# Cached latent pages loaded by SyncE, rotary products as 64x64 tiles, and paired key heads in a hybrid MLA/DSA step

## The reference, cut to what matters

```
k_nope = c_kv @ w_uk                 # 8 heads of 64, prompt: kn, kl
s = einsum('bqhc,bkc->bhqk', q_lat, c_kv) + einsum('bqhr,bkr->bhqk', q_pe, k_pe)
s = where(k_pos <= q_pos, s * MLA_SCALE, NEG_INF)     # k: 4096 cached, 8 new
p = softmax(s);  o_lat = einsum('bhqk,bkc->bqhc', p, c_kv);  o = o_lat @ w_uv
# cached c_kv (256) and k_pe (32) rows lie in pages of 128 tokens, 32 pages a batch,
# page numbers in page_table[8, 32]; branch B gathers 256 picked k and v rows a query
```

## Time and profile before

| what | value |
|---|---|
| median of three runs | 1749.62 us |
| profiled execution, its own time | 1741.32 us |
| its span | 1739.5 us |
| PE busy | 1626.2 us (93%) |
| DVE busy | 866.3 us (50%) |
| ACT busy | 421.6 us (24%) |
| POOL busy | 337.0 us (19%) |
| gate tiles on PE | 400.27 to 528.2 us |
| latent stage on PE | 531.36 to 806 us |
| DMA | 218.38 MB, mean 126 GB/s |

### The profile page before, as it was taken

How to read it: one execution, slowest core, us unless ns; L and a number is a source line. 1 busy time by engine, 2 the same in 40 slices (tenths; PEclk the granted TensorE clock), 3 DMA queues, 4 the chain that set the end, 5 groups by cost and what they waited for, 6 DMA issues and landing times.

```text
span 1739.5 us, 21664 instructions
## 1 busy us (share of the span) xinstructions
PE 1626.2 (93%) x8572; PEld 999.0 (57%) x8572; DVE 866.3 (50%) x1636; ACT 421.6 (24%) x1111; POOL 337.0 (19%) x348
## 2 busy tenths in 40 slices
PE   6999989999999898998687899999999999989998
PEld 3554444446776666665454566547777777744443
DVE  3448798998522887874877742222322323210011
ACT  2131312001015545644355531001111111100010
POOL 2000000010004777770555630000000000000000
PEclk9899989999999999998798899999999999999999
DMA  8311212142306788877555845302122122111100
GB/s 247 141 62 61 106 42 98 63 167 86 135 36 242 264 283 298 278 264 219 144 147 150 280 134 182 115 20 89 49 73 73 49 73 73 49 61 49 65 23 32
DMA packets 89846, 218.38 MB, mean 126 GB/s; under 512 B 13576, under 2 KB 37520, under 8 KB 83696
## 3 DMA queue, kind: packets, MB, share of 16 engines
q0 software_dynamic: 29168, 116.66, 20.2%
q1 hardware_dynamic: 59506, 93.24, 16.2%
q10 hardware_dynamic: 1072, 7.09, 1.4%
HBM read 199.99 MB, written 16.84 MB: 125 GB/s over the span
## 4 chain that ended last, share of the span: by engine, by line
PE 77%; DVE 9%; POOL 6%; issue 3%; DMA 3%; ACT 2%; ACTq 0%; SPq 0%; DVEq 0%
PE PS L630 13%; PE PS L2063 13%; PE PS L2108 11%; PE PS L2091 7%; PE PS L681 7%; POOL mem L1820 5%; PE PS L2040 4%; PE PS L1538 2%; PE PS L746 2%; PE PS L2017 2%; DVE mem L1732 2%; PE PS L1408 2%; DVE mem L1731 1%; PE PS L1051 1%; PE PS L2471 1%
## 5 line engine op out<-in xcount | busy, mean ns | idle before, releaser
L630 PE MATMUL PS<-mem 128*128 128x512 f32 (+3 forms) x580 | 234.8, 561 | 0.0
L2063 PE MATMUL PS<-mem 128*128 128x376 f32 x704 | 231.7, 481 | 0.0
L2108 PE MATMUL PS<-mem 128*128 128x512 f32 (+1 forms) x440 | 192.2, 599 | 1.4 <-DVE mem L2287 1.4
L2063 PEld LDWEIGHTS PS<-mem 128*128 128x128 f32 x704 | 131.0, 189 | 79.3
L630 PEld LDWEIGHTS PS<-mem 128*128 128x128 f32 (+1 forms) x580 | 100.5, 186 | 119.8 <-issue 119.5
L1820 POOL DMA_INDIRECT mem<-in_cache_dsa_k,mem x128 | 143.9, 1124 | 43.6 <-issue 38.4
L1820 POOL DMA_INDIRECT mem<-in_cache_dsa_v,mem x128 | 122.5, 957 | 145.4 <-PE PS L1520 113.1
L2108 PEld LDWEIGHTS PS<-mem 128*128 128x128 f32 (+1 forms) x440 | 80.7, 184 | 112.3 <-issue 110.7
L2091 PE MATMUL PS<-mem 128*128 128x216 f32 x704 | 135.8, 345 | 0.0
L2091 PEld LDWEIGHTS PS<-mem 128*128 128x128 f32 x704 | 129.2, 189 | 10.7
L2268 DVE TENSOR_SCALAR mem<-mem 128x528 f32<-128x528 f32 x22 | 12.2, 555 | 238.8 <-ACT mem L2171 238.8
(11 more groups left out here) (312 smaller groups left out, 2087.7 us busy)
## 6 DMA issues: line engine op xcount, KB each, us to landing
mem<-in_w_in SPq DMA_DIRECT2D x10, 2048.0 KB, 8.2
mem<-in_w_ffn_g SPq DMA_DIRECT2D x11, 1024.0 KB, 5.4
mem<-in_w_ffn_u SPq DMA_DIRECT2D x11, 1024.0 KB, 5.4
mem<-in_w_ffn_d SPq DMA_DIRECT2D x10, 1024.0 KB, 5.0
tmp_gates<-mem SPq DMA_DIRECT2D x16, 296.0 KB, 2.1
mem<-tmp_gates SPq DMA_DIRECT2D x16, 296.0 KB, 4.0
mem<-in_w_o SPq DMA_DIRECT2D x2, 2048.0 KB, 11.8
mem<-in_x_prompt SPq DMA_DIRECT2D x6, 512.0 KB, 13.6
```

Of the source, the lines that this page charges most:

```text
L630: ins = pe.matmul(PS[0:n, b[bank], out_at:out_at + width], left[:, k, cols], w[:, k, at:at + width], start=k == 0, stop=k == k_range - 1)
L2063: pe.matmul(PS[:, 3 * (f % 2) + j, 0:UP_A], w[:, k, :], h2T[:, k, 0:UP_A], start=k == 0, stop=k == KD - 1)
L2108: return pe.matmul(PS[0:TW[m], (5 * n + m) % 8, :], upT[:, f, token_cols(m)], w[:, i, :], start=f == 0, stop=f == NF - 1)
```

## The change: what it does

The page loads move from POOL to SP (`sp_kpe_load`, `sp_latent_load`): per group of 8 pages SP loads the page numbers into registers, checks their range, and issues one DMA of 16 partitions per page. Batch 0's groups stand behind gate stores 8 to 12, those of the batches 1 to 7 behind SP's sample loads. POOL keeps the k and v gathers alone. The rotary products of an odd chunk and the even one before it go through four 64x64 tiles in two phases, around the odd chunk's second half of dots. The new tokens' products of all batches are made once, in batch 0. `outputs(b-1)` come behind the second chunk, ACT's and DVE's orders follow. `kn` and `kl` take two heads at once. The wait for the gate stores is left to SP alone. Two ring slots and two reloads at the end of the stage (kT, vb) change places, and four turns of x come one unit later.

The diff, cut to its core:

```diff
-        units += [("wt", 0)] + [("kn", h) for h in range(H)] + [("kl", 0), ("ql", 0), ("ql", 1)]
+        units += [("wt", 0)] + [("kn", p) for p in range(H // 2)] + [("kl", 0), ("ql", 0), ("ql", 1)]
...
-                    ins = pe.matmul(PS[0:64, b[0], :], wuk[:, c, 64 * m:64 * m + 64], ckvT[:, c, 0:512],
+                    ins = pe.matmul(PS[:, b[0], :], wuk[:, c, 128 * m:128 * m + 128], ckvT[:, c, 0:512],
...
-        AHEAD = 3
+        AHEAD = 2
         ROWS_B = 0
-        K_FROM = 4
+        K_FROM = 1
...
-            for i in range(2):
-                eng.wait_ge(sem(f"gates_stored{i}"), upto(f"gates_stored{i}", len(gate_tiles) - 2 + i))
...
+        def sp_pages(sp, b, first, n):
+            return nc.values_load_multi_w_load_instructions(
+                I["page_table"][b:b + 1, first:first + n], engines=[mybir.EngineType.SP], min_val=0,
+                max_val=I["cache_mla_ckv"].shape[1] - 1)[1]
+        def sp_kpe_load(sp, b):
+            if b:
+                sp.wait_ge(sem("sturned"), upto("sturned", ("p", b - 1, 1)))
+            for k in range(4):
+                for i, page_no in enumerate(sp_pages(sp, b, 8 * k, 8)):
+                    src = I["cache_mla_kpe"][0, bass.ds(page_no, 1)].rearrange("o (p r) d -> (o p) (r d)", p=16)
+                    sp.dma_start(kpe_raw[16 * i:16 * i + 16, 256 * k:256 * k + 256], src).then_inc(
+                        sem("kpe_in"), tick("kpe_in", *((b,) if k == 3 and i == 7 else ()), by=16))
+        def sp_latent_load(sp, n):
+            b, k = n // 4, n % 4
             if n >= 8:
-                gp.wait_ge(sem("latents_used"), upto("latents_used", n - 8))
-            gp.indirect_dma_start(raw_slot(n), None, ckv_rows,
-                                  bass.IndirectOffsetOnAxis(ap=idx_ckv[:, b, j:j + 1], axis=0)).then_inc(
-                sem(f"ckv_in{n % 8}"), tick(f"ckv_in{n % 8}", n, by=16))
+                sp.wait_ge(sem("latents_used"), upto("latents_used", n - 8))
+            for i, page_no in enumerate(sp_pages(sp, b, 8 * k, 8)):
+                src = I["cache_mla_ckv"][0, bass.ds(page_no, 1)].rearrange("o (p r) c -> (o p) (r c)", p=16)
+                sp.dma_start(raw_slot(n)[16 * i:16 * i + 16, :], src).then_inc(
+                    sem(f"ckv_in{n % 8}"), tick(f"ckv_in{n % 8}", *((n,) if i == 7 else ()), by=16))
...
+                if i == 8:
+                    sp.wait_ge(sem("heads_stored"), upto("heads_stored"))
+                    sp_kpe_load(sp, 0)
+                if 9 <= i < 13:
+                    sp_latent_load(sp, i - 9)
...
+            wait_stored(sp, "vb")
+            for b in range(1, NB):
+                sp_kpe_load(sp, b)
+                for k in range(4):
+                    sp_latent_load(sp, 4 * b + k)
...
-            phase_a_done(pe)
+            pe.wait_ge(sem("turned_act"), upto("turned_act", "kb", 4, 0))
...
+                            ins = pe.matmul(PS[64 * u:64 * u + 64, k % 2, :], q2[f], latT(("c", b, k, u, f)), start=f == 0,
+                                            stop=False, skip_group_check=True)
+                        if k % 2 and f == 0:
+                            if k == 1:
+                                pe.wait_ge(sem("sturn_out"), upto("sturn_out", ("p", b, 1)))
+                                pe.wait_ge(sem("qpe_spread"), upto("qpe_spread", b))
+                            rotary(b, k, 0).then_inc(sem("rotary_half"), tick("rotary_half", b, k))
...
+                    if k % 2:
+                        pe.wait_ge(sem("rotary_half"), upto("rotary_half", b, k))
+                        rotary(b, k, 1).then_inc(sem("latent_dots"), tick("latent_dots", b, k))
+                        same(("latent_dots", b, k - 1), ("latent_dots", b, k))
+                    if k == 0 and b == 0:
+                        new_tokens()
...
+            def rotary(b, k, phase):
+                for q in range(2):
+                    for u in range(2):
+                        for half, r in enumerate((LO, HI)):
+                            c, i = k - 1 + (half + phase) % 2, 2 * half + q
+                            ins = pe.matmul(PS[64 * u:64 * u + 64, c % 2, 128 * i:128 * i + 128], qpe_z[r, b % 2, i, :],
+                                            kpeT[b % 2][r, 2 * c + u, :], start=False, stop=phase == 1,
+                                            skip_group_check=True)
+                return ins
...
+            def new_tokens():
+                for b in range(NB):
+                    new, q = slice(NT * b, NT * b + NT), slice(64 * b, 64 * b + 64)
+                    out = PS[0:64, 3, 64 + NT * b:64 + NT * b + NT]
+                    for f in range(2):
+                        pe.matmul(out, ql_s[:, f, q], ckv_new[:, f, new], start=f == 0, stop=False)
+                    ins = pe.matmul(out, qpe_s[0:32, q], kpe_new[0:32, new], start=False, stop=True)
+                ins.then_inc(sem("own_dots"), tick("own_dots"))
...
-        gather_times = [(5 * ((n - 8) // 4 + 1) + 3 + n % 4 / 2 if n >= 8 else 0, n, None) for n in range(3, 4 * NB)]
-        gather_times += [(max(1, K_FROM + (q - 4) * (5 * NB - K_FROM) / NS), q, q) for q in range(NS)]
-        gather_order = [x[1:] for x in sorted(gather_times, key=lambda x: (x[0], x[1]))]
...
-            for n, q in gather_order:
-                if q is None:
-                    gp_latent_load(gp, n)
-                else:
-                    gp_gather(gp, "k", q)
+            for q in range(NS):
+                gp_gather(gp, "k", q)
```

More of the change, by code:

```diff
@@ L160, in trunk @@
         idx_row = K.take(NB, dtype=U32)
-        idx_ckv = K.take(NB, 4, dtype=U32)
+        K.take(NB * 4)
         small = K.take(64)
@@ L249, in trunk @@
         vb_at = qb_at + 2 * 4 * NCOL
-        slots = [C2.take(2048) for _ in range(4)]
-        slots[3:3] = [mem[:, vb_at:vb_at + 2048]]
+        slots = [C2.take(2048) for _ in range(4)] + [mem[:, vb_at:vb_at + 2048]]
         slots += [C.take(2048) for _ in range(3)]
@@ L267, in trunk @@
         R = Region(mem, picks_at, picks_at + ROW)
+        own = mem[0:64, picks_at:picks_at + NB * NT].rearrange("p (b n) -> p b n", b=NB)
         low, up, keep, page_f, off_f = (R.take(TOPK_S) for _ in range(5))
@@ L724, in wait_stored, with gates_done @@
                 eng.wait_ge(sem(f"stored_{name}_p"), upto(f"stored_{name}_p", 4))
+        def gates_done(eng):
+            for i in range(2):
+                eng.wait_ge(sem(f"gates_stored{i}"), upto(f"gates_stored{i}", len(gate_tiles) - 2 + i))
         def phase_a_done(eng):
@@ L991, in dots @@
                         close(b - 2)
+                    if b == 0 and k == 0:
+                        wait_unit_read(pe, ("gt", len(gate_tiles) - 1))
                     if k >= 2:
@@ L1019, in dots @@
                         pe_sturn(pe, ("n", b), [phys[0:64, 128 * f:128 * f + 128] for f in range(2)], 64)
-                pe.wait_ge(sem("scored"), upto("scored", b, 2))
-                new = slice(NT * b, NT * b + NT)
-                for f in range(2):
-                    pe.matmul(PS[0:64, 0, 0:NT], q2[f], ckv_new[:, f, new], start=f == 0, stop=False)
-                pe.matmul(PS[0:64, 0, 0:NT], qpe_s[0:32, 64 * b:64 * b + 64],
-                                 kpe_new[0:32, NT * b:NT * b + NT], start=False, stop=True).then_inc(
-                    sem("latent_dots"), tick("latent_dots", b, 4))
+            def rotary(b, k, phase):
[15 more added lines that the diff above has]
+                ins.then_inc(sem("own_dots"), tick("own_dots"))
             def outputs(b):
@@ L1280, in dve_latent @@
                 row, cm, cl = row_scores[b % 2], chunk_max[:, b % 2, :], col[:, b % 2, :]
-                for c in range(5):
-                    at = 5 * b + c + 1
-                    if c == 3 and b:
+                for c in range(4):
+                    if c == 2 and b:
                         top(b - 1)
-                        divide(b - 1)
+                    at = 5 * b + {0: 2, 1: 2, 2: 5, 3: 5}[c]
                     while scored_so_far < min(NS, NS * (at - K_FROM) // (5 * NB - 2 - K_FROM)):
@@ L2365, in _ @@
             for kind in ("kb", "vb"):
-                if kind == "vb":
-                    gp.wait_ge(sem("heads_stored"), upto("heads_stored"))
-                    for n in range(3):
-                        gp_latent_load(gp, n)
                 for m in range(NTILE):
@@ L2509, in _ @@
                     pe_unit(pe, u)
-                if i == 0:
+                if i == 1:
                     for m in range(2, NTILE):
```

112 lines of the change are left out of this document (50 added, 62 removed).

## The result

The changed kernel takes 2011.65 us (median of four runs, 2004.44 to 2014.04) against 1748.08 us of the kernel before in the same session: a ratio of 1.1498, 95% interval 1.1454 to 1.1543. The prediction said 1835 us (1705 to 1905): the direction is right, the time lies outside the range.

A forecast was written before the change was run, and what follows sets the result against it. TensorE bounds the latent stage before, SP's page loads after: 555.5 + 56 groups at 6.0 us ends it at 891.5, +85.5 us; 1741.3 + 85.5 = 1827, plus 8.3 to the median gives 1835 us, range 1705 to 1905.

The forecast's parts named there:

- SP's stream sets the end: Latent stage: SP's page-load instructions set its end, 1768 to 1920 us in total; chance 0.58.
- The price of a group, g = 6.0: SP's time per group of 8 pages: 3.2 + 1.4 + 1.4 = 6.0 us, ends 3.8 and 10.1; break-even 4.47.
- the DMA issues: SP, per group: eight page DMAs at 0.40 us each, 3.2 us, bounds 2.6 and 3.4.
- rival 3: Latent stage: SP also held by its DMA queue, 7.5 to 10 us per group, 1920 to 2065 us; chance 0.10.
- The small instructions: SP, per group: 24 register instructions for range checks and addresses, 1.4 us, bounds 1.2 and 2.9.
- The register loads: SP, per group: two dependent loads of registers from memory, 1.4 us, bounds 0 and 3.8.
- Where SP starts: End of SP's sample loads, where 56 groups begin: 536.1 us before, less 9 of kn, 527.
- The gate stage: Batch 0's groups among the gate stores: taken at 0, a stall of some 4 us beginning near g = 7.
- the pairing: Key and value projection ahead of the gates: two heads per matmul in kn and kl, -9 us, bounds -5 and -10.
- The tail: Behind the last page: landing 1.9, last chunk's turn, dots and rotary about 6.5, then 20 to the sample outputs; 28.5 us.
- Rotary: Latent stage on TensorE: four 64x64 tiles beside each other halve rotary time, -8 to -14 us, -11 taken.
- Rival 1 (hidden SP): Latent stage: SP hidden, TensorE sets the pace, if g is below 4.2; total 1712 us, 1700 to 1735; chance 0.26.

The follow-up runs named there:

- the run with pages on POOL and K_FROM 4: Changed kernel with all page loads back on POOL and first k products of branch B as late as in the kernel before: 1734.28 us, 0.9938.

## Why the prediction was wrong

- **That SP's stream sets the end, and that the change is slower: right.** SP doesn't wait, TensorE waits 240 us for pages, and three runs bear it out: without the checks the time falls, with dearer issues it rises, and with a quarter of the bytes it stays. The run with shared page numbers is no such test, as a wait took the place of what it saved.
- **The price of a group, g = 6.0: wrong, 8.6.** This is the step that failed, and it is worth 56 x 2.6 = 145 us. Of its three terms the DMA issues were nearly right (0.40 taken, 0.346 at the mean), and the queue didn't hold SP as rival 3 would have it: the longest of the 512 page issues took 1.8 us. The small instructions weren't: I took 24 of them at the 0.06 us gap between two DMAs. There are 32 (each page's address takes two), and a range check is 147 ns of arithmetic besides its assert and two gaps: 2.0 us for the checks and some 1.5 for the addresses, 3.5 where I had 1.4. I had a better upper row in hand (0.12 for a semaphore wait, 2.9 in sum) and took the lower end. The register loads were 2.06 instead of 1.4; I halved a trip for which the row showed 1.5. The Trainium skill, "DMA: Bandwidth & Descriptors", Latency and other measured facts, has about 600 ns as the floor of a register load. This trace's shortest is 827: the floor holds, but it was no price to add up with. The Trainium skill, "Runtime: NRT & Kernel Launch", Instruction fetch mechanics, has about 200 ns per register even for bulk. Here eight page numbers took 900 at the median, 113 each, and the pointer alone took as long (926); the trace decides, and that this price summed to nearly the 2.06 measured is luck.
- **Where SP starts: 527 expected, 549.4 measured, 22 us.** Three parts make it up. The gate stage, which I took at 0, is 11.3 us longer: 7.9 are TensorE's waits for ACT's gate copies (2.11 and 0.53 of them in the rows above), and ACT itself waited 55.4 us for gate stores. The prediction placed such a stall near g = 7. From the last gate matmul to the end of the sample loads SP takes 15.4 us (533.97 to 549.4) where it took 8.0 (528.17 to 536.1), as three gate stores were still to go and one took 6.77 us to land. And the gates start 5.5 us sooner, not 9: 6.8 in kn's own matmuls (15.9, now 9.1), nearly nothing in kl (1.98 to 1.85: half as many matmuls of 16 columns take as long), less some 1.75 as kn starts later (256.54, now 258.29). With paired heads alone kn starts at 255.61 and the gates at 392.06, 8.2 us sooner than before (one execution each). So the pairing was priced about right, and another part of the change takes 2.7 us back ahead of kn; the moved turns of x are the likely one, but no run has them alone.
- **The tail: 28.5 expected, 39.3 measured.** From the last rotary tile to the end it is the 20 us expected. What I left out lies ahead of it: outputs(6), 9.9 us of TensorE (1033.42 to 1043.34) that stand between the last page, issued at 1030.6 and landed some 5 us later (the median is 4.8), and the turn of the last chunk at 1043.34. This isn't the price of the moved order, which I had put at 0. In the run with the page part alone, where outputs come a chunk later as before, they stand in the tail too (1045.44 to 1055.30), and the tail is 45.5 us.
- **The range.** 555.5 + 56 x 8.59 = 1037, and 22 + 11 more give the 1070 measured. With 8 us behind the stage these are, to 1 us, the 186 us by which the profiled execution (2013.33) lies above the 1827 forecast for it. g = 8.6 lay inside the bounds I had worked out (up to 10.1); rival 3, which shares that stretch but has another mechanism, had 0.10. I cut the range at g near 7.3. The bounds of three unknown terms were added, then most of their upper half was left out.
- **Rotary: -11 us of TensorE expected, 6.7 measured, hidden behind SP.** A pair of chunks took 5.5 us before (2.75 per chunk in the earlier trace rows) and takes 5.08 in the run with pages on POOL and K_FROM 4: 0.42 x 16 = 6.7. Eight rotary matmuls of 128 columns take 0.60 to 0.67 us as 64x64 tiles where they took 0.98, so not half, as I had carried over from the 512-column tiles of the earlier trace rows. And the dots, split by the first phase, take 3.89 us a pair where they took 3.54. The Trainium skill, "TensorEngine Tiling (Array Packing)", Key Properties, says that a change of tiling mode drains TensorE. Two fewer of them per pair made no difference (the run with both phases behind the dots: 0.14 us less in the dots, 0.16 more in the rotary tiles), so the runs here don't show what such a change costs; a wait between the phases came in at the same time and could hide it.
- **The prompt stage, 8.8 us longer:** not foreseen. The mean granted clock, a mix of the two levels of 1.2 and 2.4 GHz, is 0.83 there against 0.88, and TensorE is busy 9.7 us longer for the same matmuls (219.53 in 1066 to 1330, 209.79 in 806 to 1064). TensorE came out of a half-idle stage; that this is why the clock was lower was not tested.
- **Rival 1 (hidden SP) needed g under 4.2.** No run reached it with a full set of pages. With 28 groups instead of 56 SP had 135.1 us to wait, and the stage was still longer than before: the DMA engines were full, and the rest looks like the refill of the slots.

## What to carry to other kernels

When a list of addresses moves from a gather engine to a sequencer, count every instruction that the sequencer will issue, register loads and checks included, and take the upper end of each price where the trace has no row; here one indirect load of 128 rows stood for some 42 instructions of a group (2 loads, 16 for checks, 24 for pages). Then look for the second limit: what a ring of buffers does when its refill takes longer, and which partitions a transfer writes to. A row measured at 512 columns is no price for 128.

## What was not expected of the hardware

- A DMA's issue on SP took 316 ns for 16 adjacent partitions and 496 ns for 16 partitions in steps of eight.
- The transfer went the other way. By queue (packets, MB, share of 16 engines' span), before, changed and changed with spread rows, in this order:

```profile
q0 software_dynamic: 29168, 116.66, 20.2%
q1 hardware_dynamic: 59506, 93.24, 16.2%
```

```profile
q1 hardware_dynamic: 75890, 131.02, 26.0%
q0 software_dynamic: 23408, 78.91, 13.0%
```

```profile
q1 hardware_dynamic: 75890, 131.02, 19.9%
```

SP's queue gained 37.8 MB and 0.260 x 16 x 2011.5 - 0.162 x 16 x 1739.5 = 3859 us of engine time; POOL's queue gave up the same bytes and 1438 us. With spread rows SP's queue gained 0.199 x 16 x 2090.9 - 4509 = 2149. So writing to 16 adjacent partitions cost 2.7 times the DMA time of POOL's loads over 128 partitions, and spreading the rows gave back 71% of the difference, if the rest of SP's queue cost what it did before.

The size depends on what runs beside. In the two runs with latent pages alone and no checks, the same sum gives 2924 us for adjacent rows (25.2% of 16 engines' span) and 2187 for spread ones (23.1%). The spread runs also issue more slowly, but nothing here makes that the reason: without checks the changed kernel's pages follow faster (6.4 us a group) and took 3399 us (26.1%), not more than 3859.
